# A two-block fp32 transformer on one core: shift columns, the place of the last turns, two roundings, and three output pieces

## The chip, the cores and the metric

The kernel runs on one core of a Trainium2 chip. Its time is the device time in microseconds of one execution; the number given is the median of several runs. A profiled execution of the same program gives the trace. All times in the trace are microseconds from the span's start.

## What is computed

The reference is a stack of ten sublayers on 256 tokens of width 1024 (float32): six of a first block (feed-forward, mixer, feed-forward, for two layers) and four of a second (mixer, feed-forward, for two layers), then a last RMS norm. What matters here is the pattern of one sublayer:

```python
shift, scale = mod[:, j, 0], mod[:, j, 1]          # from c, one vector per layer and sublayer
h = rms(x) * g_norm[l, j] * (1.0 + scale) + shift
gu = h @ w_up; g, u = split(gu, 2)                 # feed-forward of width 2816
x = x + gate * ((silu(g) * u) @ w_down)
# a mixer: h @ w_in, a convolution and a gated recurrence (block 1), two or three
# kinds of attention of 256 tokens, their normed outputs @ w_out, added to x
...
out = rmsnorm(x, g_final)                           # after the last sublayer
```

With R the tokens' factors 1/rms(x), h = R * (x * g * (1 + scale)) + shift. So the product of h with a weight is R times the product of x * g * (1 + scale), plus the product of shift, which is the same for every token. The kernel uses this at the start of each sublayer.

## The kernel before

**Layout.** Activations are held turned: X[:, c, :] is 128 features of chunk c (eight chunks) by 256 tokens. Every matrix product is made of 128x128 blocks of weights as the stationary operand and 256 tokens as the moving one. Float32 accuracy comes from three fp32r products: each weight half panel (128x1024) is rounded into WH by ScalarE (`hi_half`, L1373) and its remainder is taken into WL by VectorE (`lo_half`, which issues through L1909); each activation likewise has a rounded part and a remainder (HH and HL for h, AH and AL for the feed-forward's hidden values, YH and YL for a mixer's output). A product takes WH x HH, WH x HL and WL x HH.

**Queues.** Each engine's program is written out by hand, in order, and all waits are explicit semaphores. SyncE loads half panels into a ring of eight slots. ScalarE rounds them (s_hi counts), VectorE makes remainders (s_lo counts), TensorE signals a finished half (s_half) and so frees the split buffer four halves later. VectorE also computes the modulation vectors from their own panels. GpSimd takes remainders of hidden values and adds squares (s_psum).

**A sublayer's start.** While the sublayer before still ends, `gained` puts x * g * (1 + scale) into HH and HL for the next one, chunk by chunk as the residual renews X. The first four weight halves are multiplied with these (`early`, `early_pair` on TensorE) before R is known. HH and HL have 320 columns a chunk: 0 to 255 are tokens, and columns 256 and 257 hold shift, HH its rounded part (L1385, ScalarE), HL its remainder (VectorE), both columns alike. These products take S + 2 = 258 moving columns. VectorE's `early` then multiplies by R and copies out the product of shift (a 128x2 copy, L1986), and ScalarE adds it: `shifted` (L1506) in the mixers. Later halves use the full h, which ScalarE's `normalised` rounds into HH and VectorE's `h_rest` takes the remainder of. There are nine such starts: each sublayer but the first.

**mixer1 on ScalarE** (subs 1 and 4) begins: high half 4, `normalised`, `shifted(0)`, high halves 5 and 6, `shifted(1)`, high half 7 (numbers within the sublayer). VectorE: `early(0)`, remainders of h, low half 5, `early(1)`, the convolution of chunk 0, low half 6, chunk 1, low half 7, chunks 2 and 3. TensorE: the four early halves, halves 4 and 5 (`columns`), half 6, two gate products, half 7.

**The down stage.** `out_proj` sums 22 blocks for each of eight chunks c; a chunk is 66 matmuls, all by L626. In the last sublayer the final norm follows: as each chunk is done, ScalarE or VectorE make XG = X * g_final (s_xg, s_xgl), and `turned_back(b)` turns XG's chunk b into tokens by two fp32 transposes (L870), into PSUM banks 6, 7, 0, 1; chunk c >= 2 is followed by `turned_back(c - 2)`.

**4-column matmuls.** `narrow` is a matmul with four stationary columns whose result nobody reads. It stands in `cols(..., paced=True)` and in `out_round`.

**Tables.** In subs 5 and 7 GpSimd fills attention tables by DMA, ScalarE rounds them in `down` (TSH at L1434, TCH at L1438, two heads a step u), GpSimd takes the remainders (L499) and then adds squares (L514).

**The end.** rs1 holds the two factors of each row; ScalarE scales the rows of tokens 0 to 127 (L1892), VectorE the others (L1906), in two pieces of 512 columns, and SyncE issues a 256 KB DMA for each (L484).

Of the kernel before, what the change touches and what calls it, by code (L numbers as in the profile page):

```python
# [15 lines left out]
KD = 8  # L16
NF = 22
EPS = 1e-6
BIG = 2.0 ** 100
# [81 lines left out]
def build(nc, A):  # L101
    ctx = ExitStack()
    with ctx:
# [347 lines left out]
        def _(e):  # L451
# [8 lines left out]
            for p, (kind, i, j) in enumerate(loads):  # L460
# [18 lines left out]
                if p == 44:  # L479
                    e.dma_start(CN[:, 0:FIRST], A["consts"][:, 0:FIRST]).then_inc(s_const_rest, 16)  # L480
            for g in range(2):
                for t, done in enumerate((s_fa, s_fd)):
                    e.wait_ge(done, g + 1)
                    e.dma_start(A["out"][128 * t:128 * t + 128, 512 * g:512 * g + 512],  # L484
                                OUT[:, t, 512 * g:512 * g + 512]).then_inc(s_out, 16)
            e.wait_ge(s_out, 64)

# [136 lines left out]
        def _(e):  # L624
# [104 lines left out]
            def early(n, p, b):  # L729

                i = 2 * UNIT0[n] + p
                wh, wl = (v3(w, KD) for w in half_of(i))
                out = PS[:, b, 0:S + 2]
                if p == 0:

                    e.wait_ge(s_x, 8 * n - 3)
                e.wait_ge(s_hi, i + 1)
                if p == 3:

                    e.wait_ge(s_lo, i + 1)  # L740
                    for k in range(KD):
                        mm(out, wh[:, k, :], HH[:, k, 0:S + 2], start=k == 0, stop=False)
                        mm(out, wh[:, k, :], HL[:, k, 0:S + 2], start=False, stop=False)
                        mm(out, wl[:, k, :], HH[:, k, 0:S + 2], start=False, stop=k == KD - 1).then_inc(s_free if k < KD - 1 else s_half, 1)
                    return
                last_chunk = KD - 1 if p == 0 else KD
                for k in range(last_chunk):
                    if p == 0:
                        e.wait_ge(s_yl, 8 * (n - 1) + k + 1)
                    mm(out, wh[:, k, :], HH[:, k, 0:S + 2], start=k == 0, stop=False)  # L750
                    if p == 1 and k == 6 and SUBS[n - 1][0] != "ffn":
                        sum_squares(n)
                    mm(out, wh[:, k, :], HL[:, k, 0:S + 2], start=False, stop=False)
                e.wait_ge(s_lo, i + 1)
                for k in range(last_chunk):
                    last = mm(out, wl[:, k, :], HH[:, k, 0:S + 2], start=False, stop=k == KD - 1)
                if p == 0:
                    if SUBS[n - 1][0] == "ffn":
                        sum_squares(n)
                    k = KD - 1  # L760
                    e.wait_ge(s_yl, 8 * n)
                    mm(out, wh[:, k, :], HH[:, k, 0:S + 2], start=False, stop=False)
                    mm(out, wh[:, k, :], HL[:, k, 0:S + 2], start=False, stop=False)
                    last = mm(out, wl[:, k, :], HH[:, k, 0:S + 2], start=False, stop=True)
                last.then_inc(s_half, 1)

            def early_pair(n):
# [5 lines left out]
                for p in range(2):  # L773
                    e.wait_ge(s_hi, h + p + 1)
                    for k in range(KD - 1):
                        if p == 0:
                            e.wait_ge(s_yl, 8 * (n - 1) + k + 1)
                        mm(outs[p], whs[p][:, k, :], HH[:, k, 0:S + 2], start=k == 0, stop=False)
                        mm(outs[p], whs[p][:, k, :], HL[:, k, 0:S + 2], start=False, stop=False)
                e.wait_ge(s_yl, 8 * n)  # L780
                for p in range(2):
                    mm(outs[p], whs[p][:, KD - 1, :], HH[:, KD - 1, 0:S + 2], start=False, stop=False)
                    mm(outs[p], whs[p][:, KD - 1, :], HL[:, KD - 1, 0:S + 2], start=False, stop=False)
                sum_squares(n)
# [96 lines left out]
            def out_proj(n, xh, xl, ready):  # L881
# [3 lines left out]
                for i in range(KD * kt):  # L885
# [7 lines left out]
                    if c == 0:  # L893
                        ready(k)
                    out = PS[:, down_bank(n, c), 0:256]
                    mm(out, wh[:, g, :], xh(k), start=k == 0, stop=False)
                    mm(out, wh[:, g, :], xl(k), start=False, stop=False)
# [7 lines left out]
                    if n == NSUB - 1 and k == kt - 1:  # L905
                        if c >= 2:
                            turned_back(c - 2)
                if n == NSUB - 1:
# [443 lines left out]
        def _(e):  # L1352
# [26 lines left out]
            def gained(m, c):  # L1379

                e.wait_ge(s_x, 8 * m - 7 + c)
                if c == 0:
                    e.wait_ge(s_ab, m)
                    shift = MOD[:, 24 * m:24 * m + 8].rearrange("p (k o) -> p k o", o=1).to_broadcast([128, KD, 2])
                    e.activation(HH[:, :, S:S + 2], shift, ACT.Copy)  # L1385
                e.activation(HH[:, c, 0:S], X[:, c, :], ACT.Copy, scale=AB[:, 8 * m + c:8 * m + c + 1]).then_inc(s_yh, 1)  # L1386
# [37 lines left out]
            def down(n):  # L1424

                for u in range(NTICK[SUBS[n][0]])[-depth_of(n) // 2:]:
# [4 lines left out]
                    if n == 5 and u in (NF + 2, NF + 3):  # L1431
                        e.wait_ge(s_toe_sa, 32)
                        for h in (0, 1) if u == NF + 2 else (2, 3):
                            e.activation(TSH[:, h, :], TSA[:, h, :], ACT.Copy).then_inc(s_toe_hi, 1)  # L1434
                    if n in (5, 7) and u in (NF + 4, NF + 5):
                        e.wait_ge(s_toe_ca, 32 if n == 5 else 64)
                        for h in (0, 1) if u == NF + 4 else (2, 3):
                            e.activation(TCH[:, h, :], TCA[:, h, :], ACT.Copy).then_inc(s_toe_hi, 1)  # L1438
# [86 lines left out]
            def mixer1(n):  # L1525
# [46 lines left out]
                hi_half(2 * u0 + 4)  # L1572
                normalised(n)
                shifted(n, 0, LX[:, 0:2, 3:259])
                hi_half(2 * u0 + 5)
                hi_half(2 * u0 + 6)
# [312 lines left out]
            e.wait_ge(s_frs, 1)  # L1889
            for g in range(2):  # L1890
                e.wait_ge(s_xt, 8 + g + 1)
                e.activation(OUT[:, 0, 512 * g:512 * g + 512], PS[:, (6, 0)[g], :], ACT.Copy, scale=rs1[:, 0:1]).then_inc(s_fa, 1)  # L1892


        @block.vector
        def _(e):
# [75 lines left out]
            def gained(m, c):  # L1972

                e.wait_ge(s_yh, 8 * m - 7 + c)
                if c == 0:
                    shift = MOD[:, 24 * m:24 * m + 8].rearrange("p (k o) -> p k o", o=1).to_broadcast([128, KD, 2])
                    tt(HL[:, :, S:S + 2], shift, HH[:, :, S:S + 2].bitcast(F32), ALU.subtract)
                stt(HL[:, c, 0:S], X[:, c, :], AB[:, 8 * m + c:8 * m + c + 1], HH[:, c, 0:S].bitcast(F32), ALU.mult,
                    ALU.subtract).then_inc(s_yl, 1)

            def early(n, u, out):
# [3 lines left out]
                b = PS[:, 2 + 2 * u:4 + 2 * u, :]  # L1985
                e.tensor_copy(SM_[:, 160 + 2 * u:162 + 2 * u].rearrange("p (a o) -> p a o", o=1), b[:, :, S:S + 1])  # L1986
                tt(out, b[:, :, 0:S], R.rearrange("p (o s) -> p o s", o=1).to_broadcast([128, 2, S]), ALU.mult).then_inc(s_early, 1)
# [554 lines left out]
            e.wait_ge(s_frs, 1)  # L2542
            for g in range(2):
                e.wait_ge(s_xt, 8 + g + 1)
                ts(OUT[:, 1, 512 * g:512 * g + 512], PS[:, (7, 1)[g], :], rs1[:, 1:2], None, ALU.mult, None).then_inc(s_fd, 1)

# [172 lines left out]
```

## Time and profile before

| | |
|---|---|
| median of three runs | 1555.13 us (1553.96 to 1555.85) |
| profiled execution | 1553.34 us |
| its span, first to last instruction | 1551.5 us |
| mean granted TensorE clock | 0.999 |
| TensorE busy | 1531.4 us, 99% of the span |
| VectorE, ScalarE, GpSimd busy | 1294.4, 911.6, 282.0 us |
| DMA | 402 MB, mean 259 GB/s |

The page's parts are: busy time by engine, a strip of 40 slices, the DMA queues, the chain of work that ended last, the costliest groups of instructions, and the DMA issues. In a timeline each row has a start, a time, the engine, the line, the operation, out<-in with the shape, and a count where neighbours alike are merged. Matmuls overlap in the pipeline, so a record of one (0.28 us) is longer than the distance to the next start; the rate is read from starts. Brackets hold the engine's idle time and what ended it.

### The profile page before, as it was taken

The numbers are of one execution on the slowest core, as the hardware profiler recorded it, in microseconds if no ns is written. First come the engines' busy times: TensorE is split into PE (matmuls) and PEld (weight loads), VectorE is DVE, ScalarE is ACT, GpSimd is POOL, SyncE is SP. The second block draws the span as 40 slices with busy tenths as digits, with TensorE's granted clock in tenths as the row PEclk, the third lists the DMA queues.
The fourth block names the chain that finished last, engine by engine and source line by source line (L and its number), as shares of the span: only waits on it lengthen the run. The fifth ranks groups of instructions, "written<-read, shape, count | busy, mean of one in ns | idle before, by whom it ended". The sixth has DMA issues, their size and how long they took to land.

```text
span 1551.5 us, 32204 instructions
## 1 busy us (share of the span) xinstructions
PE 1531.4 (99%) x13130; PEld 1512.1 (97%) x13130; DVE 1294.4 (83%) x1943; ACT 911.6 (59%) x1584; POOL 282.0 (18%) x288
## 2 busy tenths in 40 slices
PE   6999999999999999999999999999999999999998
PEld 6999999999999999999999999999999999999998
DVE  7998898997898888888998889889888889885553
ACT  6555468765555545459765455677555466765453
POOL 4322000112210222000113242101222201021100
PEclk9999999999999999999999999999999999999999
DMA  9999974479987899864579998445999963567761
GB/s 366 363 375 335 316 254 163 164 251 324 321 319 265 300 312 324 300 231 164 177 251 332 314 335 286 150 137 164 321 329 332 332 233 123 167 207 239 239 209 42
DMA packets 110612, 401.99 MB, mean 259 GB/s; under 512 B 12450, under 2 KB 12706, under 8 KB 110336
## 3 DMA queue, kind: packets, MB, share of 16 engines
q1 hardware_dynamic: 109136, 395.34, 73.2%
q0 software_dynamic: 1328, 4.58, 0.9%
q8 instruction: 104, 1.70, 0.4%
q14 instruction: 44, 0.36, 0.1%
HBM read 398.83 MB, written 1.05 MB: 258 GB/s over the span
## 4 chain that ended last, share of the span: by engine, by line
PE 88%; DVE 5%; ACT 4%; DMA 1%; issue 1%; DVEq 0%; SPq 0%; ACTq 0%
PE PS L626 87%; DVE WL L1909 2%; ACT WH L1373 1%; DMA ring<-in_up 1%; DVE SCR L1909 1%; DVE SCR L1912 1%; DVE SCR L2293 1%; DVE SMALL L2292 0%; ACT SCR L1701 0%; DVE ring L1935 0%; DMA ring<-in_ada 0%; PE PS L1215 0%; PE PS L827 0%; DVE SMALL L2332 0%; ACT HH L1405 0%
## 5 line engine op out<-in xcount | busy, mean ns | idle before, releaser
L1909 DVE TENSOR_TENSOR WL<-ring,WH 128x1024 fp32r<-128x1024 f32 (+1 forms) x502 | 603.5, 1236 | 151.9 <-ACT WH L1373 151.4
L626 PE MATMUL PS<-HH,WH 128*128 128x256 f32 (+2 forms) x2600 | 617.6, 279 | 1.9 <-DVE WL L1909 1.2
L626 PE MATMUL PS<-HL,WH 128*128 128x256 f32 (+1 forms) x2592 | 602.1, 277 | 0.0
L1373 ACT ACTIVATE WH<-ring 128x1024 fp32r<-128x1024 f32 (+1 forms) x502 | 507.0, 1050 | 44.2 <-PE PS L626 36.0
L626 PEld LDWEIGHTS PS<-HH,WH 128*128 128x128 f32 (+1 forms) x2600 | 488.2, 188 | 3.8 <-issue 2.6
L626 PEld LDWEIGHTS PS<-HL,WH 128*128 128x128 f32 x2592 | 481.1, 188 | 0.5
L626 PE MATMUL PS<-HH,WL 128*128 128x256 f32 (+1 forms) x2592 | 372.0, 277 | 0.4
L1935 DVE CUSTOM_DVE_ANT_0 ring<-ring,CB,VC 128x1024 f32<-128x1024 f32 x240 | 331.3, 1397 | 3.2 <-DMA ring<-in_ada 3.2
L626 PEld LDWEIGHTS PS<-HH,WL 128*128 128x128 f32 x2592 | 332.1, 188 | 1.3 <-DVE WL L1909 1.1
L626 PE MATMUL PS<-AH,WH 128*128 128x256 f32 x1056 | 292.4, 277 | 0.0
L626 PE MATMUL PS<-AH,WL 128*128 128x256 f32 x1056 | 292.1, 277 | 0.2 <-DVE WL L1909 0.2
L626 PE MATMUL PS<-AL,WH 128*128 128x256 f32 x1056 | 292.0, 277 | 0.0
L583 POOL TENSOR_TENSOR AL<-SCR,AH 128x256 fp32r<-128x256 f32 x132 | 154.9, 1176 | 554.1 <-ACT AH L1444 554.1
L626 PEld LDWEIGHTS PS<-AH,WL 128*128 128x128 f32 x1056 | 198.7, 188 | 0.4 <-DVE WL L1909 0.4
L626 PEld LDWEIGHTS PS<-AL,WH 128*128 128x128 f32 x1056 | 198.2, 188 | 0.0
L626 PEld LDWEIGHTS PS<-AH,WH 128*128 128x128 f32 x1056 | 198.2, 188 | 0.0
L1444 ACT ACTIVATE AH<-SCR 128x256 fp32r<-128x256 f32 x132 | 55.1, 419 | 223.5 <-DVE SCR L1909 216.7
L514 POOL TENSOR_TENSOR SQ<-SQ 128x256 f32<-128x256 f32 x69 | 59.1, 856 | 472.8 <-ACT SQ L1389 469.7
L1386 ACT ACTIVATE HH<-X,AB 128x256 fp32r<-128x256 f32 x72 | 36.4, 505 | 103.9 <-DVE X L1912 103.5
L1448 ACT ACTIVATE SCR<-PS 128x256 f32<-128x256 f32 x122 | 46.3, 381 | 72.7 <-PE PS L626 72.7
L626 PE MATMUL PS<-SCR 128*128 128x64 f32 (+6 forms) x528 | 76.6, 314 | 0.0
L1912 DVE SCALAR_TENSOR_TENSOR X<-PS,MOD,X 128x256 f32<-128x256 f32 x112 | 52.9, 477 | 28.0 <-PE PS L626 27.9
(257 smaller groups left out, 1535.0 us busy)
## 6 DMA issues: line engine op xcount, KB each, us to landing
ring<-in_up SPq DMA_DIRECT2D x176, 512.0 KB, 5.7
ring<-in_ada SPq DMA_DIRECT2D x144, 512.0 KB, 6.1
ring<-in_ffn SPq DMA_DIRECT2D x132, 512.0 KB, 4.9
ring<-in_mod SPq DMA_DIRECT2D x96, 512.0 KB, 6.0
ring<-in_down SPq DMA_DIRECT2D x88, 512.0 KB, 5.8
ring<-in_win SPq DMA_DIRECT2D x64, 512.0 KB, 5.5
ring<-in_wout SPq DMA_DIRECT2D x32, 512.0 KB, 4.4
ring<-in_winv SPq DMA_DIRECT2D x8, 512.0 KB, 4.2
```

The lines of the kernel that those rows point to most:

```text
L514: e.tensor_tensor(SQ[:, c, :], SQ[:, c - 1, :], SQ[:, c, :], ALU.add).then_inc(s_psum, 1)
L583: e.tensor_tensor(AL[:, f, :], G6[:, 3 + f % 3, :], AH[:, f, :].bitcast(F32), ALU.subtract).then_inc(s_al, 1)
L626: return e.matmul(out, lhsT, rhs, start=start, stop=stop, skip_group_check=skip)
L1373: e.activation(half_of(i)[0], slot_of(("half", i, 0))[:, 0:w], ACT.Copy).then_inc(s_hi, 1)
L1386: e.activation(HH[:, c, 0:S], X[:, c, :], ACT.Copy, scale=AB[:, 8 * m + c:8 * m + c + 1]).then_inc(s_yh, 1)
L1444: e.activation(AH[:, f, :], G6[:, 3 + f % 3, :], ACT.Copy).then_inc(s_ah, 1)
L1448: e.activation(G6[:, f % 3, :], PS[:, up_bank(f), 0:256], ACT.Silu).then_inc(s_silu, 1)
L1909: return e.tensor_tensor(out, a, b, op)
L1912: return e.scalar_tensor_tensor(out=out, in0=a, scalar=s, in1=b, op0=op0, op1=op1)
L1935: ins = e.tensor_tensor_reduce(out=w, in0=w, in1=CB[:, :], scale=1.0, scalar=bias, op0=ALU.mult, op1=ALU.add, accum_out=MOD[:, 2 * i + j:2 ...
L2293: step(e.match_replace(WK[t][:, 0:m], m8, src, LOWEST))
```

## The change

Five things are done:

1. In the early products the shift's rounded part goes to column 256 of HH and its remainder, rounded, to column 257 of HH. HL has no shift columns, and its early matmuls take 256 moving columns. VectorE's `early` adds the two product columns in a reduction where it copied one.
2. In the last down stage `turned_back(0)` to `turned_back(4)` all follow chunk 6, and `turned_back(5)` follows chunk 7. A `narrow` matmul stands ahead of block k = 2 of chunk 7.
3. The rounding of table TCH comes one step earlier in `down` of subs 5 and 7.
4. In mixer1 ScalarE rounds half 5 ahead of `shifted(0)`.
5. The output goes out in pieces of 256, 256 and 512 columns: six DMAs.

```diff
+PIECES = ((0, 256), (256, 256), (512, 512))
...
-            for g in range(2):
+            for g, (at, w) in enumerate(PIECES):
                 for t, done in enumerate((s_fa, s_fd)):
                     e.wait_ge(done, g + 1)
-                    e.dma_start(A["out"][128 * t:128 * t + 128, 512 * g:512 * g + 512],
-                                OUT[:, t, 512 * g:512 * g + 512]).then_inc(s_out, 16)
-            e.wait_ge(s_out, 64)
+                    e.dma_start(A["out"][128 * t:128 * t + 128, at:at + w], OUT[:, t, at:at + w]).then_inc(s_out, 16)
+            e.wait_ge(s_out, 32 * len(PIECES))
...
# early, and alike in early_pair (every matmul on HL)
                         mm(out, wh[:, k, :], HH[:, k, 0:S + 2], start=k == 0, stop=False)
-                        mm(out, wh[:, k, :], HL[:, k, 0:S + 2], start=False, stop=False)
+                        mm(out[:, 0:S], wh[:, k, :], HL[:, k, 0:S], start=False, stop=False)
                         mm(out, wl[:, k, :], HH[:, k, 0:S + 2], start=False, stop=k == KD - 1).then_inc(s_free if k < KD - 1 else s_half, 1)
...
# out_proj
+                    if n == NSUB - 1 and c == KD - 1 and k == 2:
+                        narrow(PS[:, 1, 256:512], AH[:, 0, :])
                     mm(out, wh[:, g, :], xh(k), start=k == 0, stop=False)
...
                     if n == NSUB - 1 and k == kt - 1:
-                        if c >= 2:
-                            turned_back(c - 2)
+                        for b in {KD - 2: range(5), KD - 1: (5,)}.get(c, ()):
+                            turned_back(b)
...
# gained, ScalarE
-                    shift = MOD[:, 24 * m:24 * m + 8].rearrange("p (k o) -> p k o", o=1).to_broadcast([128, KD, 2])
-                    e.activation(HH[:, :, S:S + 2], shift, ACT.Copy)
+                    e.activation(HH[:, :, S:S + 1], MOD[:, 24 * m:24 * m + 8].rearrange("p (k o) -> p k o", o=1), ACT.Copy)
...
# down, ScalarE
-                    if n in (5, 7) and u in (NF + 4, NF + 5):
+                    if n in (5, 7) and u in (NF + 3, NF + 4):
                         e.wait_ge(s_toe_ca, 32 if n == 5 else 64)
-                        for h in (0, 1) if u == NF + 4 else (2, 3):
+                        for h in (0, 1) if u == NF + 3 else (2, 3):
...
# mixer1, ScalarE
                 normalised(n)
+                hi_half(2 * u0 + 5)
                 shifted(n, 0, LX[:, 0:2, 3:259])
-                hi_half(2 * u0 + 5)
                 hi_half(2 * u0 + 6)
...
# the end, ScalarE; VectorE alike
-            for g in range(2):
-                e.wait_ge(s_xt, 8 + g + 1)
-                e.activation(OUT[:, 0, 512 * g:512 * g + 512], PS[:, (6, 0)[g], :], ACT.Copy, scale=rs1[:, 0:1]).then_inc(s_fa, 1)
+            for at, w in PIECES:
+                e.wait_ge(s_xt, 8 + at // 512 + 1)
+                e.activation(OUT[:, 0, at:at + w], PS[:, (6, 0)[at // 512], at % 512:at % 512 + w], ACT.Copy, scale=rs1[:, 0:1]).then_inc(s_fa, 1)
...
# gained and early, VectorE
-                    shift = MOD[:, 24 * m:24 * m + 8].rearrange("p (k o) -> p k o", o=1).to_broadcast([128, KD, 2])
-                    tt(HL[:, :, S:S + 2], shift, HH[:, :, S:S + 2].bitcast(F32), ALU.subtract)
+                    shift = MOD[:, 24 * m:24 * m + 8].rearrange("p (k o) -> p k o", o=1)
+                    tt(HH[:, :, S + 1:S + 2], shift, HH[:, :, S:S + 1].bitcast(F32), ALU.subtract)
...
-                e.tensor_copy(SM_[:, 160 + 2 * u:162 + 2 * u].rearrange("p (a o) -> p a o", o=1), b[:, :, S:S + 1])
+                e.tensor_reduce(SM_[:, 160 + 2 * u:162 + 2 * u], b[:, :, S:S + 2], AX.X, ALU.add)
```

## Rows read from the trace of the kernel before

**Rows 1.** The page, busy times: busy us, share of the span, instructions.

```profile
PE 1531.4 (99%) x13130; PEld 1512.1 (97%) x13130; DVE 1294.4 (83%) x1943; ACT 911.6 (59%) x1584; POOL 282.0 (18%) x288
```

**Rows 2.** Timeline of TensorE around the first turn of the last stage.

```profile
1502.03 0.28 PE L626 MATMUL PS<-AH,WH 128*128 128x256 f32 x1
...
1503.05 0.28 PE L626 MATMUL PS<-AH,WH 128*128 128x256 f32 x1
...
1504.08 0.38 PE L870 MATMUL PS<-identr,SCR 128*128 128x128 f32 x2
1504.22 0.36 PE L626 MATMUL PS<-AH,WH 128*128 128x256 f32 x1
...
1505.01 0.28 PE L626 MATMUL PS<-AH,WH 128*128 128x256 f32 x1
...
1506.07 0.28 PE L626 MATMUL PS<-AH,WH 128*128 128x256 f32 x1
```

**Rows 3.** Chain that ended last, last stage: start, us, what; five such pairs.

```profile
1504.46 7.78 PE PS L626 x66
1512.24 0.22 PE PS L870 x2
```

**Rows 4.** Timeline of TensorE, early stage of sub 2, matmuls of 258 columns.

```profile
308.22 0.28 PE L626 MATMUL PS<-HH,WH 128*128 128x258 f32 x1
...
311.84 0.28 PE L626 MATMUL PS<-HH,WH 128*128 128x258 f32 x1
```

**Rows 5.** Waits of TensorE's weight loads, 215 to 232: us, times, longest.

```profile
PEld PS L626 <- DVE WL L1909: 0.3, 1, 0.3
PEld PS L626 <- DVE SCR L1912: 0.2, 1, 0.2
```

**Rows 6.** Timeline of TensorE behind a turn and a 4-column matmul, two mixers.

```profile
294.43 0.28 PE L626 MATMUL PS<-YH,WH 128*128 128x256 f32 x1
...
295.49 0.28 PE L626 MATMUL PS<-YH,WH 128*128 128x256 f32 x1
...
1054.68 0.36 PE L626 MATMUL PS<-YH,WF 128*4 128x256 f32 x1
...
1055.58 0.28 PE L626 MATMUL PS<-YH,WH 128*128 128x256 f32 x1
...
1056.60 0.28 PE L626 MATMUL PS<-YH,WH 128*128 128x256 f32 x1
```

**Rows 7.** Chain that ended last, 215 to 232, start of the first mixer1.

```profile
218.30 0.80 ACT SCR L1506 x2
...
220.08 0.04 DVE WL L1909
...
223.86 1.14 DVE WL L1909
```

**Rows 8.** Timeline of TensorE, halves 5 and 6 of the first mixer1.

```profile
220.12 0.37 PE L626 MATMUL PS<-HH,WH 128*128 128x256 f32 x1
...
224.64 0.28 PE L626 MATMUL PS<-HL,WH 128*128 128x256 f32 x1
225.05 1.21 PE L626 MATMUL PS<-HH,WL 128*128 128x256 f32 x8
```

**Rows 9.** Timeline of ScalarE, the third gate's output in mixer1.

```profile
235.34 1.70 ACT L1538 ACTIVATE SCR<-PS,VC 128x256 f32<-128x256 f32 x4 [2.99 <-PE PS L626]
```

**Rows 10.** DMA issues, 897 to 915 (KB, us to landing), and ScalarE's timeline, sub 5.

```profile
SCR<-in_carel POOLq DMA_DIRECT2D x1, 256.0 KB, 11.2
...
912.96 0.71 ACT L1434 ACTIVATE TH<-SCR 128x256 fp32r<-128x256 f32 x2
...
921.38 0.51 ACT L1386 ACTIVATE HH<-X,AB 128x256 fp32r<-128x256 f32 x1 [4.12 <-DVE X L1912]
```

**Rows 11.** SyncE's issues at the end, and GB/s from 1547 in slices of 0.125.

```profile
1547.12 1.83 SPq L484 DMA_DIRECT2D out<-SCR  x4
...
GB/s 0 0 0 0 0 0 0 98 328 442 344 442 393 410 426 377 442 377 426 377 442 377 426 394 393 459 344 459 213 0 0 0 0 0 0 0 0 0 0 0
```

## What I predicted, and how

> **What bounds the kernel.** I read the page first: its busy times and its chain. TensorE is busy 99% of the span [rows 1], and the chain is nearly all its own. So an edit pays only if it takes time from TensorE's row of matmuls, or from the few places where that row waits. Next I read TensorE's instructions one by one, start against start, since the durations of pipelined matmuls overlap. Plain 256-column matmuls come in two paces: nine of them take 1502.03 to 1503.05, 0.1133 us each; after two fp32 turns at 1504.08 nine take 1505.01 to 1506.07, 0.1178 us each [rows 2]. The granted clock is 0.999 over the whole span, the 2.4 GHz level, so the clock doesn't make the difference. The slow pace stays: the chain shows 66 matmuls in 7.78 us for each of the last five chunks [rows 3], 66 x 0.1178, where 66 x 0.1133 is 7.48. Matmuls of 258 columns are slower still: 30 starts from 308.22 to 311.84, 0.1207 us each [rows 4]. Last, the waits: TensorE loses 0.3 us on a remainder (WL) and 0.2 us on the convolution in the first mixer of kind 1 [rows 5], and as much in the second.
>
> My sums start from the profiled execution: 1553.34 us, span 1551.5 and 1.8 around it. The median of three runs is 1.8 us above it, inside their 1553.96 to 1555.85; I carry the difference over to the median.
>
> **Part 1: turns in one place.** In the last down stage each of chunks 2 to 6 is followed by two fp32 turns; now the turns 0 to 4 all come after chunk 6, turn 5 after chunk 7 as before. Chunks 3 to 6, 4 x 66 = 264 matmuls, then follow fp32r matmuls only, and should keep the pace of chunks 0 to 2: 264 x (0.1178 - 0.1133) = 1.17 us. The turns themselves save nothing. A pair costs the chain 0.22 [rows 3], five pairs 1.10; in a row they start some 0.11 apart (the record of two is 0.38 long, of one 0.27) and only the last pays for the change back, some 1.1 again. Their inputs are long there (XG 4 needs chunk 4, two chunks back), and s_xt is wanted only after the end of the stage.
>
> A 4-column matmul comes in at chunk 7, k = 2. The trace has it both ways right behind turns: at 1054.68 the pace was 0.113 again some four matmuls later (nine from 1055.58 to 1056.60); in the first mixer it stayed 0.118 (nine from 294.43 to 295.49) [rows 6]. Here six matmuls lie between turns and it. If it works, 56 of the remaining 60 gain 0.0045, 0.25, less its own 0.12: 0.13 us. If not, it costs 0.12. I take 0.13.
>
> **Part 2: two columns of HH.** Of each early stage's 96 matmuls the 32 on HL shrink from 258 to 256 columns; nine stages, 288 matmuls. The trace never shows 256 columns between 258. Ends: nothing (the pair keeps 0.1207), and 0.1133, which gives 288 x 0.0074 = 2.13 us. I take the slow 256 pace, the nearest row: slow 256s never recovered by themselves in 264 matmuls. 288 x 0.0029 = 0.84 us. A loss is possible too (rivals). What the trace says against plain counting: two columns more cost 0.0029 even against the slow pace.
>
> The Trainium skill, "TensorE: Matmul & The Clock Gate", section Back-to-back issue gap, puts a warm gap at N/2.4 + 2.5 ns, so by N alone; at its figure two columns are worth 0.8 ns, an estimate of 0.24 us for this part. No row here follows it: 256 columns stand at both 0.1133 and 0.1178.
>
> The rest of part 2 is small. ScalarE's copy of shift halves its columns and waits for the residual anyway; VectorE's subtraction keeps its place. VectorE's copy of two numbers in each early() becomes a sum over two pairs: no row shows such a sum; I take it between nothing and 0.1 us more. It lies on part 3's path once in each of two mixers, under a slack of 0.5 us there: nothing.
>
> **Part 3: a rounding moved.** In mixer1 ScalarE now does the high half 5 ahead of shifted(0), not behind. The chain names every link [rows 7]: shifted 218.30 (0.80), the high half behind it, its remainder on VectorE 220.08, then early(1), conv(0), the remainder of half 6 from 223.78 to 225.00, then TensorE. Without the 0.80 and a wait of some 0.1, half 5 is ready at 219.2, and all behind it is 0.9 earlier. What is queued behind is safe: conv(0) wants shifted(0), which now ends at about 220.2, before VectorE gets there (221.0); half 6 begins on ScalarE at 220.2 as before. TensorE gets back:
> - at 220.12 a record of 0.37 instead of 0.28, a wait for half 5: 0.09;
> - from 224.64 to 225.05 0.41 instead of 0.11, 0.30, and behind it a record of 1.21 for eight, where one of 0.28 and seven paces of 0.113 are 1.07: 0.44 in all. The remainder would come at 224.1, wanted at 224.6;
> - before the second gate 0.2 on the weight-load side, of which I count half: 0.1, since the matmul ahead covers the rest.
>
> Together some 0.6, twice 1.20 us [rows 5, 8]. Is it given back? Downstream ScalarE becomes the chain, and TensorE waits at 258; but that queue starts with the gates' output at 235.34, after 2.99 us of idling for TensorE [rows 9]. It starts 0.6 earlier too, so the gain stays. Bounds: 0.4 (the remainder still late) to 1.3.
>
> **Part 4: tables sooner.** Two times 0.71 us of ScalarE move one step ahead in subs 5 and 7. The cover is ScalarE's idling in that stage, 4.12 us before 921.38, ahead of the place where they stood; uncovered it would be 0.7 us. They may not come before their tables: issued around 901, landed 11.2 us later, 912, while the rounding ahead of the new place starts at 912.96 and takes 0.71 [rows 10]. GpSimd gets to its square sums earlier, for which TensorE does not wait. Nothing.
>
> **Part 5: three pieces.** The first piece is 256 columns: half of the 512 columns for which the engines take about 0.7, so the first DMA is issued 0.3 us earlier. But SyncE needs 1.83 us for four issues, 0.46 each, and now has six: the last is issued at 1546.8 + 5 x 0.48 = 1549.2 instead of 1548.5. Before, the 1 MB flowed from 1547.95 to 1550.6 without a break, 0.85 behind the first issue; the fourth DMA had slack [rows 11]. If bandwidth rules, the end comes 0.3 earlier; if issues rule, the fifth (issued 1548.7) flows from about 1549.6, and the two large ones need half of the 1 MB's 2.65: 1550.9, 0.3 later. I take 0.1 later, nearer to the issues, whose row is plain. The last engine piece ends 0.3 later on either engine, in time for its issue.
>
> **Sum:** 1.17 + 0.13 + 0.84 + 1.20 - 0.10 = 3.24 us. 1553.34 becomes 1550.1, the median 1555.13 becomes 1551.9, 0.21% less.
>
> **Rivals.**
> - A: among 258s the 256s run at 0.1133, part 2 is 2.13: 4.5 us, 1550.6. For it: fast matmuls stay fast if nothing disturbs them. Against: one 258 after another disturbs.
> - B: part 2 gives nothing and the remainder of half 6 is still late (part 3 is 2 x 0.2): 1.6 us, 1553.5. For it: every pattern of 258s seen is slow whatever its operands.
> - C: the pace has nothing to do with the turns or the pattern; columns alone count. Part 1 loses 0.12 and part 2 gives at most 288 x 2/258 of 0.1207, 0.27: 1.25 us with parts 3 and 5, 1553.9. Against it: the pace changes in the very place of a turn [rows 2]. By the Trainium skill's formula it would be 1553.9 too.
> - D, slower: a change of width between neighbours costs what the change from fp32 back to fp32r costs, 0.36 - 0.28 = 0.08 us [rows 2]. Alternating widths bring about 64 changes a stage, 576 in all: 46 us, less the other parts' 2.4, 1598.7. It decides from 0.01 us a change (5.8 in all, 3.4 slower). Against: the first 258 behind 256s, at 308.22, has a plain 0.28 [rows 4].
>
> **Chances.** Forecast 0.58, A 0.15, B 0.18, C 0.05, D 0.04. Predicted 1551.9. Part 2's ends and the run-to-run spread of some 1 us make the range 1550.0 to 1553.6, which leaves out C, D and the tails. 0.2% (3.1 us) is about what a measurement can tell from no change. The forecast lies on that line: a little over half of it and all of A are faster, 0.47; the rest, B and C 0.49 same; D 0.04 slower.
>
> **What would show it.** Chunks 3 to 6 in 7.48 us each with no turn between; 0.113 in chunk 7 some ten matmuls in; early stages 0.8/9 = 0.09 us shorter, HL starts 0.118 apart; no gap at 220.1 and 224.6; the last packet within 0.3 us of where it stood relative to the engines. A slow chunk 3, a 258/256 pair over 0.242, or a wait for half 6 would prove me wrong.

## The result: 1.07% slower, because three feed-forwards run at the slow pace

The changed kernel takes 1571.5 us (median of 4 runs, 1570.9 to 1572.0) where the kernel before takes 1554.6 (4 runs, 1554.0 to 1555.9): ratio 1.0107, 95% interval 1.0095 to 1.0119. The profiled execution took 1570.94 us; its span is 1569.1 where before has 1551.5, 17.6 us more.

The page of after, busy times, answers to [rows 1]; below it the view of the cores, with the span and the granted clock.

```profile
PE 1549.2 (99%) x13131; PEld 1530.4 (98%) x13131; DVE 1296.6 (83%) x1944; ACT 912.6 (58%) x1585; POOL 281.1 (18%) x288
```

```profile
core 0: 1569.1 us, clock 0.999
```

TensorE grew by 17.8 us, by about as much as the span, at the same clock and with one instruction more. So it is not waits that grew: the same matmuls stand farther apart. Where, the windows view tells: busy time and number of TensorE's matmuls in three stretches inside the feed-forwards of subs 3, 7 and 9 (a sub is a sublayer, counted from 0). First before, then after:

```profile
510.00:660.00 150.00, 150.00 (x1326) 1.00 0.90 313
1090.00:1240.00 150.00, 150.00 (x1326) 1.00 0.93 329
1390.00:1490.00 100.00, 100.00 (x884) 1.00 0.73 239
```

```profile
510.00:660.00 150.00, 150.00 (x1276) 1.00 0.88 303
1090.00:1240.00 150.00, 150.00 (x1276) 1.00 0.91 316
1390.00:1490.00 100.00, 100.00 (x851) 1.00 0.71 235
```

150 us hold 1326 matmuls before, one in 0.1131 us, and 1276 after, one in 0.1176: the two paces of [rows 2], but now the slow one for a whole feed-forward. The other feed-forwards don't show it throughout. From one early stage's first 258-column matmul to the next (timelines of both kernels; one decimal):

| stretch | before, us | after, us | difference |
|---|---|---|---|
| start to sub 1 | 205.2 | 204.7 | -0.5 |
| sub 1 and sub 4, the mixers of [rows 5] | 103.0, 103.0 | 102.9, 102.5 | -0.1, -0.5 |
| sub 2, feed-forward | 180.9 | 181.1 | +0.1 |
| sub 3, feed-forward | 180.8 | 187.2 | **+6.4** |
| sub 5, feed-forward | 181.5 | 182.2 | +0.7 |
| subs 6 and 8, mixers | 112.7, 112.7 | 112.6, 112.6 | -0.1, -0.1 |
| sub 7, feed-forward | 180.8 | 187.2 | **+6.4** |
| sub 9 and the end | 190.8 | 196.1 | **+5.3** |

TensorE's program ahead of sub 1 is the same in both, and over the 17 profiles of this document that stretch lies between 204.7 and 206.5 us, so a difference of 0.5 there says nothing. The three large ones begin at one place, the 4-column matmul behind the early stage. TensorE's timeline there, sub 3, before and then after (start, duration, instruction):

```profile
501.06 0.28 PE L626 MATMUL PS<-HH,WL 128*128 128x258 f32 x1
501.18 0.28 PE L626 MATMUL PS<-HH,WF 128*4 128x256 f32 x1
501.30 0.28 PE L626 MATMUL PS<-HH,WH 128*128 128x256 f32 x1
501.42 0.28 PE L626 MATMUL PS<-HH,WL 128*128 128x256 f32 x1
501.54 0.28 PE L626 MATMUL PS<-HH,WH 128*128 128x256 f32 x1
501.65 0.28 PE L626 MATMUL PS<-HH,WL 128*128 128x256 f32 x1
501.77 0.28 PE L626 MATMUL PS<-HH,WH 128*128 128x256 f32 x1
501.88 0.28 PE L626 MATMUL PS<-HH,WL 128*128 128x256 f32 x1
501.99 0.28 PE L626 MATMUL PS<-HH,WH 128*128 128x256 f32 x1
```

```profile
500.35 0.28 PE L626 MATMUL PS<-HH,WL 128*128 128x258 f32 x1
500.46 0.28 PE L626 MATMUL PS<-HH,WF 128*4 128x256 f32 x1
500.58 0.28 PE L626 MATMUL PS<-HH,WH 128*128 128x256 f32 x1
500.70 0.28 PE L626 MATMUL PS<-HH,WL 128*128 128x256 f32 x1
500.81 0.28 PE L626 MATMUL PS<-HH,WH 128*128 128x256 f32 x1
500.93 0.28 PE L626 MATMUL PS<-HH,WL 128*128 128x256 f32 x1
501.05 0.28 PE L626 MATMUL PS<-HH,WH 128*128 128x256 f32 x1
501.17 0.28 PE L626 MATMUL PS<-HH,WL 128*128 128x256 f32 x1
```

Before, the starts fall from 0.12 apart to 0.11 within four matmuls. After, they stay at 0.12 (0.118 in the mean), and nothing changes that until the next early stage (in sub 9, until chunk 7 of the down stage). Nothing waits in either. Call an early stage mixed when matmuls of 256 columns stand among those of 258, as part 2 has it. In subs 2, 4, 6 and 8 of after, the same pair of a mixed stage and a 4-column matmul ended in the fast pace. So the first question was which part does it, the second what makes this place different.

### The profile page after: what moved, and what is told of

The parts are those of the page before. It is cut to its first block, busy times and chain, and to the rows that moved or that the text cites. A ratio compares the mean times of both kernels' runs of the same rounds, so it can differ in the third digit from the quotient of the medians.

```text
span 1569.1 us, 32210 instructions
## 1 busy us (share of the span) xinstructions
PE 1549.2 (99%) x13131; PEld 1530.4 (98%) x13131; DVE 1296.6 (83%) x1944; ACT 912.6 (58%) x1585; POOL 281.1 (18%) x288
## 4 chain that ended last, share of the span: by engine, by line
PE 90%; DVE 6%; ACT 3%; issue 1%; DMA 1%; SPq 0%; DVEq 0%; ACTq 0%
PE PS L626 89%; DVE WL L1910 1%; DVE ring L1936 1%; ACT WH L1375 1%; DMA ring<-in_ada 1%; DVE SCR L2294 1%; DVE SCR L1910 1%; DVE SMALL L2293 0%; DVE SCR L1913 0%; DVE SMALL L2335 0%; PE PS L827 0%; PE PS L1217 0%; ACT SCR L1702 0%; DVE SMALL L2333 0%; ACT SCR L1602 0%
## 5 line engine op out<-in xcount | busy, mean ns | idle before, releaser
L626 PE MATMUL PS<-HH,WH 128*128 128x256 f32 (+2 forms) x2600 | 624.8, 280 | 1.9 <-DVE WL L1910 1.1
L626 PE MATMUL PS<-HL,WH 128*128 128x256 f32 x2592 | 609.1, 279 | 0.0
L626 PE MATMUL PS<-HH,WL 128*128 128x256 f32 (+1 forms) x2592 | 376.1, 279 | 0.1
L626 PEld LDWEIGHTS PS<-HH,WL 128*128 128x128 f32 x2592 | 335.5, 188 | 0.6 <-DVE WL L1910 0.5
L1913 DVE SCALAR_TENSOR_TENSOR X<-PS,MOD,X 128x256 f32<-128x256 f32 x112 | 53.0, 477 | 33.7 <-PE PS L626 33.6
```

Source lines behind the costliest of these rows:

```text
L626: return e.matmul(out, lhsT, rhs, start=start, stop=stop, skip_group_check=skip)
L1913: return e.scalar_tensor_tensor(out=out, in0=a, scalar=s, in1=b, op0=op0, op1=op1)
```

## Experiments

Medians and ratios are against the kernel before on the same chip; "in subs 3, 7, 9" means the three windows above.

### Which part: part 2 alone, and everything but part 2

p2_only is the kernel before with part 2 of the diff alone. 

> The kernel before with part 2 alone: the matmuls of the remainder in the early stages 256 instead of 258 columns wide, both parts of Shift in HH. First theory (phase): the loss comes with part 2, and not in the early stages themselves: they get shorter by about 0.1 us each, but the single 4-column matmul behind them no longer gives the fast pace back in three feed-forwards (subs 3, 7 and 9), whose some 1500 matmuls of 256 columns each then stand 0.1177 us apart instead of 0.1133: 1500 x 0.0044 = 6.6 us each, so 15 to 20 us over the kernel before, ratio 1.010 to 1.013. Rival (mixed widths cost by themselves): the early stages of the trace are longer than the 11.9 us of before, and the paces behind them are as before. Rival (another part is responsible, as the moved rounding, the earlier tables or the turns): the time is within 2 us of before, at or under 1554.6 us.

no_p2 is the changed kernel with part 2's edits alone undone. 

> The changed kernel with part 2 alone undone (258 columns again in the matmuls of the remainder). First theory (phase): the fast pace is back in subs 3, 7 and 9, and what is left are the other parts of the prediction, 1.17 + 0.13 + 1.20 - 0.1 = 2.4 us under the kernel before: 1552.2 us, ratio 0.9985. Rival (another part is responsible): about 1571 us, with three feed-forwards at 0.1177 us.

Measured: p2_only 1571.8 us, ratio 1.0111 (1.0098 to 1.0125), and 1276, 1276 and 851 matmuls in subs 3, 7, 9. no_p2 1552.6 us, 0.9989 (0.9980 to 0.9998), with 1326, 1326 and 884. Part 2 carries the whole loss. Its own stages are not longer: from the first 258-column matmul to the 4-column one behind, sub 3 has 12.03 us before (489.15 to 501.18) and 11.85 in after (488.61 to 500.46), and eight of the nine stages stand like that. The ninth, in sub 2, takes 12.18 us in after, with a wait of 0.3 us at its start for a remainder by VectorE (HL, L1913); before_none, whose stages have 258 columns throughout, has it there too (12.37 us). The rival of a cost inside the mixed widths falls.

### What the 4-column matmul does there

A feed-forward works in units f of two weight halves. Units 0 and 1 are its early stage, and the 4-column matmul stands at the start of unit 2, straight behind it. two_narrow has a second one, a unit later, in every feed-forward:

```diff
-                paced = (4, 5, 7) if n == 0 else (2, 3) if SUBS[n - 1][0] == "mix1" else (2,)
+                paced = (4, 5, 7) if n == 0 else (2, 3)
```

> The changed kernel with a second 4-column matmul, one unit later (f = 3), in every feed-forward and not only behind the first mixer. First theory (phase): the second one meets the stream in another phase, and where it works the units behind it run at 0.1133 us: 1551 to 1556 us if it works in all three, and about 6 us more for each in which it fails too. Rival (the slow pace has to do with where data or weights lie, or with 256 columns standing among 258): the second one changes nothing, 1571 us.

before_none is the kernel before without the one at f = 2 in subs 3, 7 and 9:

```diff
-                paced = (4, 5, 7) if n == 0 else (2, 3) if SUBS[n - 1][0] == "mix1" else (2,)
+                paced = (4, 5, 7) if n == 0 else (2, 3) if SUBS[n - 1][0] == "mix1" else ()
```

> The kernel before without the 4-column matmul behind the early stage of subs 3, 7 and 9 (those that do not follow the first mixer). First theory (phase): these matmuls are what gives the fast pace back in before, and without them the three feed-forwards run at 0.1177 us: the same 15 to 20 us over before, ratio 1.010 to 1.013, with the same picture by sub as the changed kernel. Rival: the pace comes back by itself, and the time is within 1 us of before; then the failing 4-column matmul cannot be what the changed kernel lost.

Measured: two_narrow 1553.8 us, 0.9994 (0.9985 to 1.0003); the second one restores the fast pace in all three. before_none 1554.2 us, 0.9999 (0.9989 to 1.0008): my first theory held that the 4-column matmul gives the fast pace back in before, and that fell. Behind a stage of 258 columns throughout the pace falls to 0.113 by itself; there the 4-column matmul changes nothing. So in after it is perhaps not too weak but harmful. after_none makes the same edit to the changed kernel. 

> The changed kernel without the 4-column matmul at f = 2 of subs 3, 7 and 9. In the kernel before, taking these away changed nothing (1554.2 against 1554.4 us): behind an early stage of 258 columns throughout, the 256-column matmuls fall to 0.113 us within four of them by themselves. Theory A (what counts is the order of widths in which the stage ends; the 4-column matmul behind a mixed stage is only too weak): behind the mixed stage the pace stays at 0.118 us without it too, 1571 us, ratio 1.010 to 1.012. Theory B (the 4-column matmul behind a mixed stage is what throws the stream into the slow pace): without it the three feed-forwards run at 0.113 us, 1551 to 1554 us.

Measured: 1552.2 us, 0.9984 (0.9975 to 0.9993). Theory B. TensorE's timeline of after_none, sub 3, behind the same mixed stage:

```profile
500.89 0.28 PE L626 MATMUL PS<-HH,WL 128*128 128x258 f32 x1
501.00 0.28 PE L626 MATMUL PS<-HH,WH 128*128 128x256 f32 x1
501.12 0.28 PE L626 MATMUL PS<-HH,WL 128*128 128x256 f32 x1
501.23 0.28 PE L626 MATMUL PS<-HH,WH 128*128 128x256 f32 x1
501.35 0.28 PE L626 MATMUL PS<-HH,WL 128*128 128x256 f32 x1
501.46 0.28 PE L626 MATMUL PS<-HH,WH 128*128 128x256 f32 x1
501.57 0.28 PE L626 MATMUL PS<-HH,WL 128*128 128x256 f32 x1
501.69 0.28 PE L626 MATMUL PS<-HH,WH 128*128 128x256 f32 x1
```

The fast pace is there from the first matmul. One 4-column matmul, put in to give it back, took it away for 170 us, three times.

### How little of the stage it takes

tail_258 keeps part 2 but gives the remainder's matmuls of the last of the four halves 258 columns again (their two columns are zeros):

```diff
-                        mm(out[:, 0:S], wh[:, k, :], HL[:, k, 0:S], start=False, stop=False)
+                        mm(out, wh[:, k, :], HL[:, k, 0:S + 2], start=False, stop=False)
...
+                    tt(HL[:, :, S:S + 1], shift, shift, ALU.subtract)
+                    tt(HL[:, :, S + 1:S + 2], shift, shift, ALU.subtract)
```

> The changed kernel with 258 columns again in the remainder matmuls of the last of the four halves of the early stages alone (24 matmuls of 258 in a row at the end of each stage of that form; the two columns of the remainder are zeros, so the sums stay the same; two small VectorE operations more per feed-forward). Theory A: the stage ends as in the kernel before, the pace behind it falls to 0.1133 us in subs 3, 7 and 9, and of the width gain three quarters are kept: 1551 to 1554 us. Theory B (the history of the whole stage counts, or something else in part 2, as the place of the columns): 0.1177 us stays, 1571 us.

tail_one differs from it in one matmul of each stage, the last but one:

```diff
-                        mm(out, wh[:, k, :], HL[:, k, 0:S + 2], start=False, stop=False)
+                        w = S + 2 if k < KD - 1 else S
+                        mm(out[:, 0:w], wh[:, k, :], HL[:, k, 0:w], start=False, stop=False)
```

> The kernel of tail_258 with one matmul per early stage back at 256 columns: the remainder matmul of the last chunk, the last but one of the stage. If it is the spacing of the very last matmuls ahead of the 4-column one that decides (Theory B1), this one change brings the slow pace back behind it in subs 3, 7 and 9 and costs 15 to 20 us: 1568 to 1572 us. If it takes the order of widths of a longer stretch (Theory B2), the time stays that of tail_258, 1552.5 us.

Measured: tail_258 1552.5 us, 0.9985 (0.9976 to 0.9994); tail_one 1572.6 us, 1.0114 (1.0099 to 1.0130), with 1276, 1276 and 851 matmuls in subs 3, 7, 9. Two columns of one matmul per stage cost 20 us. tail_one, sub 3:

```profile
501.06 0.28 PE L626 MATMUL PS<-HL,WH 128*128 128x256 f32 x1
501.19 0.28 PE L626 MATMUL PS<-HH,WL 128*128 128x258 f32 x1
501.30 0.28 PE L626 MATMUL PS<-HH,WF 128*4 128x256 f32 x1
501.42 0.28 PE L626 MATMUL PS<-HH,WH 128*128 128x256 f32 x1
501.53 0.28 PE L626 MATMUL PS<-HH,WL 128*128 128x256 f32 x1
501.65 0.28 PE L626 MATMUL PS<-HH,WH 128*128 128x256 f32 x1
501.77 0.28 PE L626 MATMUL PS<-HH,WL 128*128 128x256 f32 x1
501.89 0.28 PE L626 MATMUL PS<-HH,WH 128*128 128x256 f32 x1
```

tail_one_none is tail_one with the edit of before_none. 

> The kernel of tail_one (one matmul of 256 columns, the last but one, among the last 24 of the stage) without the 4-column matmul at f = 2 of subs 3, 7 and 9. Theory B (the narrow end of the stage alone does no harm; it is the 4-column matmul behind such an end that does): 0.1133 us in the three feed-forwards, 1552 us. Rival (one 256-column matmul at the end of a stage is enough for the slow pace by itself): 1570 us or above.

Measured: 1552.8 us, 0.9989 (0.9980 to 0.9999). The narrow matmul at the end does no harm alone; only the pair with the 4-column matmul does.

### Its place, and its weight load

narrow_late is the changed kernel with the 4-column matmul of subs 3, 7 and 9 eight matmuls further on, at k = 4 of the same unit; its output goes to another PSUM bank, as its old one is being summed into there. 

> The changed kernel with the 4-column matmul of subs 3, 7 and 9 moved: not straight behind the early stage but 8 matmuls of 256 columns later. Theory B (the stream falls to 0.113 us by itself behind the mixed stage, and the 4-column matmul does harm only where it follows the stage directly): at its new place it meets a stream at 0.113 us, where the trace of before has such matmuls without effect (325.84 us), and the time is that of after_none, 1552.2 us. Rival (a 4-column matmul does harm anywhere in this order of weight loads): 1571 us.

full_width replaces it, at its old place, by an ordinary matmul:

```diff
-                    narrow(out, HH[:, 0, 0:S])
+                    if n in (3, 7, 9):
+                        mm(out, wh[:, 0, :], HH[:, 0, 0:S])
+                    else:
+                        narrow(out, HH[:, 0, 0:S])
```

> The changed kernel with an ordinary matmul (128 columns of weights, 256 moving) in place of the 4-column one at f = 2 of subs 3, 7 and 9; its product is overwritten. Theory C1 (it is the short weight load of the 4-column matmul that sets the stream off behind the mixed stage): the ordinary one does no harm, and the time is that of after_none plus 3 x 0.11 us, 1552.5 us. Theory C2 (any one matmul more shifts the phase in which the weight loads stand): 1571 us.

Measured: narrow_late 1552.9 us, 0.9986 (0.9977 to 0.9996), full_width 1553.2 us, 0.9991 (0.9982 to 1.0000), both with 1326, 1326 and 885 matmuls in the windows. In a stream already at 0.113 the 4-column matmul does nothing, and an ordinary matmul in its place does nothing either. What sets the stream off is the 4-column matmul with its weight load of four columns, straight behind the mixed stage. Its four output rows and the tile WF that its weights come from go along with the load and weren't parted from it, and of the places behind the stage only the first and the ninth were tried.

### The other parts by themselves

> The kernel before with part 1 alone (turns of the last down stage in one place and a 4-column matmul in chunk 7). By the prediction chunks 3 to 6 of the last down stage take 7.48 us each instead of 7.78 and the time falls by 1.17 to 1.30 us: 1553.1 us, ratio 0.9992. Rival (a part of the 2.4 us expected of no_p2, of which 1.8 were measured, is missing here): chunk 7 or the turns cost 0.6 us more than worked out, and the ratio is 0.9996 or above.

> The kernel before with part 3 alone (the rounding of half 5 ahead of the shifted copy in the first mixer). By the prediction it removes waits of TensorE at 220.1, 224.6 and 225 us of 0.6 us in each of two mixers: 1553.2 us, ratio 0.9992. Rival: the waits go, and the phase in which the later stream stands gives part of it back (another pace in some stretch behind it): 1554.4 us within 0.4.

> The kernel before with parts 4 and 5 alone (tables rounded one unit sooner, output in three pieces). By the prediction a loss of 0.1 us at the end and nothing else: 1554.8 us, ratio 1.0001. Rival (the earlier rounding of the tables gets in the way of what ScalarE owes TensorE): waits of TensorE behind 912 us, over 1555.5 us.

Measured: p1_only 1553.7 us, 0.9995 (0.9986 to 1.0004); p3_only 1554.1 us, 0.9996 (0.9987 to 1.0005); p45_only 1555.8 us, 1.0006 (0.9997 to 1.0015). All three lie above what was expected, p3_only within its rival's 1554.4 us and p45_only over its rival's 1555.5. Their medians alone settle little; the traces say more, below. p45_only's 1.0 us has no new wait in it: half is part 5, and in its profile sub 5 ran slow behind the wait told of under part 4 (182.2 us instead of 181.5). Whether its other runs did too isn't shown, nor whether the earlier tables make it likelier: four of the 12 profiles with part 4 ran slow there, and one of the five without.

### A kernel that beats both

none_all is the changed kernel without any 4-column matmul straight behind an early stage:

```diff
-                paced = (4, 5, 7) if n == 0 else (2, 3) if SUBS[n - 1][0] == "mix1" else (2,)
+                paced = (4, 5, 7) if n == 0 else (3,) if SUBS[n - 1][0] == "mix1" else ()
...
# columns, the mixers
-                cols(2 * UNIT0[n] + 2 * u, n, PS[:, b, 0:256], u == 2, u == 2)
+                cols(2 * UNIT0[n] + 2 * u, n, PS[:, b, 0:256], u == 2)
```

> The changed kernel without any 4-column matmul straight behind an early stage: in the feed-forwards (those behind the first mixer keep the one at f = 3) and in the mixers. In after_none these stages of subs 1, 2, 4, 5 and 8 go over from 0.113 us ahead to 0.118 us behind. Theory B: without it they go over to 0.113 us by themselves, which gives some 60 to 80 matmuls x 0.0044 = 0.3 us in each of three mixers and 0.3 in each of two feed-forwards, 1.5 us: 1550.7 us, ratio 0.9974. Rival: behind a mixer the stream is met in another phase, and single ones turn slow: 1552 to 1558 us.

none_two is none_all with part 5 undone, `PIECES = ((0, 512), (512, 512))`. 

> The kernel of none_all (1550.8 us) with part 5 undone (output in two pieces). From the start of the scalings at the end to the end of the span the traces have 5.05 us with two pieces and 5.55 us with three, six issues of SyncE taking 2.84 us where four take 1.83: 0.5 us less than none_all, 1550.3 us, ratio 0.9971. Rival (the 1.0 us that p45_only lay over the kernel before came from the tables, part 4): 5.5 us from the scalings to the end here too, and no gain against none_all.

Measured: none_all 1550.8 us, 0.9974 (0.9963 to 0.9984); none_two 1549.5 us, 0.9967 (0.9954 to 0.9979), 22 us under the changed kernel. Both came within a microsecond of what was expected. For none_all that was in part luck. Behind the early stages of subs 1, 2, 4, 5 and 8 its pace is 0.113, as expected, but the expectation left out that six matmuls go, of 0.12 us each, 0.7 us. And the stretches got shorter by less than the 0.3 us set down for each: against after_none subs 1 and 4 by 0.1 and 0.2 us, and sub 2 not at all, since a wait of 0.2 us for a remainder by VectorE (HL, L1913) comes up behind its early stage.

## Why the prediction was wrong, step by step

I predicted 1551.9 us, in 1550.0 to 1553.6, and 0.04 for slower. It came to 1571.5.

**The step that failed** is one that was never written down for part 2: that what stands behind an early stage stays as it was. I priced the 288 narrower matmuls where they stand and left their neighbour out, though my own [rows 6] showed a 4-column matmul ending both ways, once at 0.113 and once at 0.118. I weighed that for the one that the change adds and not for the nine whose surroundings it alters. A term was due: about 1500 matmuls between two early stages, 0.0044 each, 6.5 us a feed-forward, and a chance that some of the nine fail. Five did, three of them with nothing behind that repaired it.

**Rival D** had the right sign by the wrong mechanism. The changes of width between neighbours cost nothing where they stand; the mixed stage is the shorter one. C is refuted too: the same 256 columns stand at either pace for 170 us. The Trainium skill, "TensorE: Matmul & The Clock Gate", section Back-to-back issue gap, also says that in a stream of weight loads and matmuls both set the spacing; full_width against the changed kernel agrees, since there only the weight load's width differs (with its source and the rows that it feeds). Its N/2.4 + 2.5 ns, which I used, is its figure for an isolated matmul; at 256 columns it gives an estimate of 0.109 us, which neither pace reached.

**Part 1, right.** Behind the down stage's chunk 6 there are ten turns in a row, then six slow matmuls, then the 4-column one and the fast pace. p1_only's chain of the end answers to [rows 3]:

```profile
1494.92 40.24 PE PS L626 x355
1535.16 1.09 PE PS L870 x10
1536.25 7.65 PE PS L626 x67
```

The ten turns take 1.09 us, as worked out; 355 matmuls ahead of them are one piece at 0.1133. From the 4-column matmul behind sub 9's early stage to the last 256-column matmul the timelines have 171.23 us before and 169.91 in p1_only: 1.32, and 1.17 + 0.13 were predicted. In after it worked as well, in chunk 7; chunks 3 to 6 didn't take 7.48 each, since the whole sub had been slow since 1384.84.

**Part 2, mis-sized where it stands.** 12.03 to 11.85 us is 0.18 for 32 matmuls, 0.0056 each, where I took 0.0029 with 0.0074 as the end: 1.6 us over nine stages instead of 0.84, a little over halfway to rival A.

**Part 3: right where it acts, in part given back behind it.** The waits of [rows 5, 8] are gone; p3_only's chain has one piece of TensorE where [rows 7] went through ScalarE and VectorE:

```profile
214.99 20.39 PE PS L626 x165
```

From the stage's start (205.24 before, 205.70 in p3_only) to the first matmul of 4 columns behind the first gate products (228.03 and 227.86) it is 22.79 and 22.16 us: 0.63 less, 0.6 predicted. But before, the group of small matmuls that begins there ended in the fast pace; with the wait gone it ends in the slow one: from there to the next gate products (234.28 and 234.34) it is 6.25 us before and 6.48 in p3_only. So 0.4 is left by then. In the second such mixer of this profile 102.97 us became 102.59, the same 0.4. In the first nothing is left at its end, 102.98 and 103.01 us: before, the slow pace behind its last 4-column matmul (294.24) went over to the fast one near 299, and in p3_only it stayed until sub 2. I argued that the gain stays since ScalarE's queue starts 0.6 earlier; no wait took it back, but changes of pace did, the term that part 2 lacked too.

**Part 4, right as far as seen.** No wait follows the earlier rounding, and sub 7 takes 180.8 us in p45_only as in before. One effect I hadn't seen: TensorE waits once in sub 5's down stage, for a remainder by VectorE. The chains of before, then of after:

```profile
936.45 1.69 DVE WL L1909
938.18 21.89 PE PS L626 x186
```

```profile
936.86 1.15 DVE WL L1910
938.05 22.06 PE PS L626 x185
```

With the tables sooner it comes some 5.5 us earlier within the sub (159.8 us behind its start where it was 165.3) and is 0.04 us shorter: start to start 0.45 to 0.47 us in the 12 profiles with part 4, 0.48 to 0.52 in the five without.

**Part 5, mis-sized.** I took 0.1 us and 0.3 as its bound. The end of none_all with three pieces and of none_two with two (rows of ScalarE, VectorE and SyncE's queue):

```profile
1544.36 1.42 ACT L1893 ACTIVATE SCR<-PS,SMALL 128x256 f32<-128x256 f32 x3
1544.36 1.54 DVE L1907 TENSOR_SCALAR SCR<-PS,SMALL 128x256 f32<-128x256 f32 x3 [1.29 <-ACT SMALL L1889]
1544.86 2.84 SPq L485 DMA_DIRECT2D out<-SCR  x6
```

```profile
1542.69 1.26 ACT L1893 ACTIVATE SCR<-PS,SMALL 128x512 f32<-128x512 f32 x2
1542.69 1.41 DVE L1907 TENSOR_SCALAR SCR<-PS,SMALL 128x512 f32<-128x512 f32 x2 [1.29 <-ACT SMALL L1889]
1543.40 1.83 SPq L485 DMA_DIRECT2D out<-SCR  x4
```

From the scalings' start to the end of the span it is 5.5 us with three pieces (1549.9) and 5.0 with two (1547.7); p45_only against before gives the same half microsecond. The first issue comes 0.2 us sooner, not 0.3, and the last one ends 0.8 us later (3.34 against 2.54 behind the scalings' start). The issues rule, as far as the small pieces go: between these p45_only's flow falls to 58 to 74 GB/s, where [rows 11] show no break, and the two large ones follow back to back. The two ends that I had drawn, 0.3 us either way, both lay too low.

**What of it can be added up.** none_two keeps parts 1 to 4: 1.3 + 1.6 + 2 x 0.4 = 3.7 us, and its span is 3.8 under before's. They agree by luck, for it also lacks nine 4-column matmuls of 0.12 us each, which makes 4.8. Of the 1.0 us that isn't there 0.4 is in sub 2, 181.0 us where it was 180.9 and 0.3 less was due, and 0.2 in sub 5: TensorE waits 0.2 us there for VectorE's HL, as in none_all. Another 0.4 is the stretch ahead of sub 1, which varies by more than that. no_p2 should have 1.3 + 0.8 - 0.5 = 1.6; 1.8 were measured.

**What stays open.** Why the pair of a mixed stage and a 4-column matmul ends slow in subs 1, 3, 5, 7 and 9 of after (in sub 5 the second one, at f = 3, restores the pace) and fast in subs 2, 4, 6 and 8. There the stages entered at 0.113 are the ones that end slow, but p2_only has one entered at 0.118 that ends slow as well (sub 7), so this is not the whole rule. Nor is the size of a wait: behind the one in sub 5 the pace was 0.118 in five of 17 profiles, after and p1_only among them, after 470 and 504 ns, and 0.113 in p3_only after 512 and in none_all after 470. Each slow one costs some 0.7 us until the next early stage. Together with the 1.8 us by which the stretch ahead of sub 1 varies, this blurs every comparison below a microsecond here.

## What to carry to other kernels

Before pricing an edit in a row of back-to-back matmuls, measure start to start what follows it, for as long as it follows: where a stream has two steady paces, an edit is worth what it does to the pace behind it, and 288 matmuls made shorter can slow 4400. A trick that restores a pace holds for the neighbours it was found with; test it again, and test leaving it out, each time the widths ahead of it change. Count the issues of a queue before splitting a transfer at the end.

## What the hardware showed that I had not expected

- The fast pace comes back by itself: behind 258 columns throughout, and behind a mixed stage too, the first 256-column matmuls were at 0.113 within four. I had only seen slow ones stay slow.
- Behind a matmul with a 4-column weight load 0.118 can turn to 0.113 (before, 1055; after, 1554.24), the pace can be 0.118 where it is 0.113 without it (after, 500.46, against after_none), or nothing changes (narrow_late). An ordinary matmul at that place does nothing.
- At either pace the stream is regular for some 1500 matmuls at a granted clock of 0.999: starts 113 or 114 ns apart (before, 510 to 660 us), or 117 to 119 (after, the same window). The two lie 0.0044 us apart, 4%.
- 256-column matmuls between 258-column ones save 0.0056 us each, more than the 0.0029 us by which the slow 256 pace lies under the 258 one.
